# The seven-product form of the up-projection in an encoder block on Trainium2: block products through sums of weights and inputs, the down-projection as a phase of its own

## What is computed

```
h = rms_norm(x, ffn_pre_g[l]) * (1.0 + scale2) + shift2
u = depthwise_conv_centred(h @ w_up[l], conv_w[l], conv_b[l])
a, bval = jnp.split(u, 2, axis=-1)
y = (jax.nn.gelu(a, approximate=True) * bval) @ w_down[l]
x = x + gate2 * rms_norm(y, ffn_post_g[l])
```

## Time and profile before

| | us |
|---|---|
| median of 3 runs | 3207.35 |
| lowest and highest | 3206.72 and 3211.47 |
| profiled execution, span | 3209.9 |

### The profile page before, as it was taken

One profiled execution on the slowest core, in us unless ns is written; L12 is line 12 of the kernel. 1 busy time (PEld: TensorE's weight loads), 2 busy tenths in 40 slices (PEclk: granted clock), 3 DMA queues, 4 the chain that ended last, 5 costly groups with the idle time before them and its releaser, 6 DMA issues.

```text
span 3209.9 us, 35608 instructions
## 1 busy us (share of the span) xinstructions
PE 3146.2 (98%) x14057; PEld 2544.4 (79%) x14057; DVE 2398.0 (75%) x2650; ACT 1274.2 (40%) x1669; POOL 206.1 (6%) x291
## 2 busy tenths in 40 slices
PE   7999999999999999989999999999999999999997
PEld 7777777777788888878888888888888888888886
DVE  5679687774699999986664567676778677777778
ACT  4433111112899999944333422222223322122123
POOL 0011431441000000000000000000000000000001
PEclk8999999999999999999999999999999999999999
DMA  8633333215411121277777221221217111111123
GB/s 321 214 145 131 122 111 109 86 63 194 154 37 37 34 55 39 73 209 215 234 226 266 95 64 49 58 61 46 64 43 256 49 58 49 43 64 43 43 64 126
DMA packets 140806, 349.34 MB, mean 109 GB/s; under 512 B 27192, under 2 KB 36408, under 8 KB 136152
## 3 DMA queue, kind: packets, MB, share of 16 engines
q1 hardware_dynamic: 123040, 303.02, 29.8%
q10 hardware_dynamic: 12096, 25.17, 2.2%
q0 software_dynamic: 5504, 18.88, 1.5%
HBM read 249.56 MB, written 92.20 MB: 106 GB/s over the span
## 4 chain that ended last, share of the span: by engine, by line
PE 53%; DMA 2%; DVE 1%; ACT 0%; issue 0%; POOL 0%; POOLq 0%; SPq 0%; ACTq 0%; DVEq 0%
PE second_ps_a L90 12%; PE second_ps_a L92 12%; PE second_ps_a L91 12%; PE second_ps_b L90 6%; PE second_ps_b L92 6%; PE second_ps_b L91 6%; DMA scratch_h<-merge_x 1%; DMA ffn_x<-scratch_x 0%; DMA merge_x<-in_w_out 0%; PE second_ps_b L1753 0%; DMA merge_st_b<-scratch_rec 0%; DVE second_y L2516 0%; POOL second_y L2345 0%; DVE second_y L2472 0%; ACT merge_x L1768 0%
## 5 line engine op out<-in xcount | busy, mean ns | idle before, releaser
L2472 DVE TENSOR_TENSOR second_y<-second_y,second_ps_b 128x512 f32<-128x512 f32 x654 | 443.5, 687 | 209.4 <-PE second_ps_b L92 209.3
L90 PE MATMUL second_ps_a<-second_h_hi,up_wu_hi 128*128 128x512 f32 x1408 | 547.9, 389 | 0.0
L91 PE MATMUL second_ps_a<-second_h_lo,up_wu_hi 128*128 128x512 f32 x1408 | 547.8, 389 | 0.0
L92 PE MATMUL second_ps_a<-second_h_hi,up_wu_lo 128*128 128x512 f32 x1408 | 547.7, 389 | 0.0
L1525 DVE TENSOR_TENSOR att_prob_lo<-att_prob,att_prob_hi 128x1024 fp32r<-128x1024 f32 x256 | 309.9, 1221 | 24.0 <-ACT att_prob_hi L1484 22.8
L92 PEld LDWEIGHTS second_ps_a<-second_h_hi,up_wu_lo 128*128 128x128 f32 x1408 | 264.3, 188 | 54.9
L90 PEld LDWEIGHTS second_ps_a<-second_h_hi,up_wu_hi 128*128 128x128 f32 x1408 | 264.3, 188 | 54.9 <-DVE up_wu_lo L2179 0.2
L91 PEld LDWEIGHTS second_ps_a<-second_h_lo,up_wu_hi 128*128 128x128 f32 x1408 | 264.3, 188 | 54.8
L90 PE MATMUL second_ps_b<-ffn_wd_hi,ffn_g_hi 128*128 128x512 f32 x704 | 274.9, 391 | 1.8 <-DVE second_y L2472 1.8
L92 PE MATMUL second_ps_b<-ffn_wd_hi,ffn_g_lo 128*128 128x512 f32 x704 | 274.6, 390 | 0.0
L91 PE MATMUL second_ps_b<-ffn_wd_lo,ffn_g_hi 128*128 128x512 f32 x704 | 274.6, 390 | 0.0
(11 more groups left out here) (289 smaller groups left out, 6255.0 us busy)
## 6 DMA issues: line engine op xcount, KB each, us to landing
up_w_st<-in_w_up SPq DMA_DIRECT2D x88, 512.0 KB, 5.9
ffn_wd_st<-in_w_dn SPq DMA_DIRECT2D x44, 512.0 KB, 3.6
scratch_gates<-proj_out SPq DMA_DIRECT2D x64, 256.0 KB, 2.0
early_w_st<-in_w_branch SPq DMA_DIRECT2D x32, 512.0 KB, 6.6
merge_gate<-scratch_gates SPq DMA_DIRECT2D x64, 256.0 KB, 4.4
scratch_h<-merge_x ACTq DMA_DIRECT2D x48, 256.0 KB, 3.8
first_raw_lo<-in_w_ada SPq DMA_DIRECT2D x17, 512.0 KB, 6.6
first_raw_lo<-in_w_ada SPq DMA_DIRECT2D x8, 1024.0 KB, 13.6
```

Of the source, the lines that this page charges most:

```text
L90: pe.matmul(out, w_hi, x_hi, start=first, stop=False)
L91: pe.matmul(out, w_hi, x_lo, start=False, stop=False)
L92: return pe.matmul(out, w_lo, x_hi, start=False, stop=last)
L2472: dve.tensor_tensor(at, at, ps_d[:, q % 4, :], ALU.add).then_inc(s_y, 1)
```

## The change

**Seven products.** A pass's result is a 2 x 2 block product: two groups of 128 output channels, two halves of the depth (512 each), two blocks of 512 positions. `UpWeights` and `UpInput` form sums of the blocks: S1 to S4 of the weights, T1 to T4 of the input. Seven products of 4 depth steps (`product`, 7 x 4 x 3 = 84 matmuls) take the place of eight.

**Weights.** The four sums are made by POOL in every pass, 128 x 512 each (`wu.add`). The seven blocks are split in four groups: A (A11 and A12), S12, S34 and LAST (A22). There is one buffer for the split weights: a group for the next pass is written when this pass's last product that reads it is done (`USED_BY`). The raw weights also have one buffer: SP loads those of the next pass when all four groups of this pass are split.

**Input.** `h` goes through DRAM as one part. The T sums and the splits of the seven input blocks are made once for each half: for the first while the mixing phase ends and in pass 0, by DVE, ACT and POOL (four sums and seven splits of 128 x 2048), for the second in pieces during the first down-projection phase.

**Results.** The seven products are put together: ACT copies two (P1, P5), DVE adds five from PSUM (`take_u2`, `take_c11`, `take_u3`, `take_c12`, `take_c21`), POOL adds two in SBUF (`take_u4`, `take_c22`). `take_c12` waits for POOL's `take_u4`. The first tap of the convolution goes from DVE to ACT (`tap`).

**Down-projection.** The gated values are stored to DRAM (`store_g`). After the 22 passes of a half its down-projection runs in blocks of 4, 3 (first half), 3, 3 and 3 tiles (second half). A block has 11 groups; a group takes two chunks of 128 channels, with two loads of `w_dn` of 512 KB, two loads of gated values, and 12 matmuls for each tile. PSUM keeps the sum over a whole block, so `add_tile` goes. `norm_tile` reads PSUM; its result and `x1` have rings of two buffers, and their stores and loads are issued by POOL.

```diff
+    A11, S1, S2, A12, S3, S4, A22 = range(7)
+    MANY = 7
+    A, S12, S34, LAST = range(4)
+    GROUP_OF = (A, S12, S12, A, S34, S34, LAST)
+    SLOTS_OF = (slice(0, 4, 3), slice(1, 3), slice(4, 6), slice(6, 7))
+    USED_BY = (3, 2, 5, 6)
+    GROUPS = 4
...
+    def load(self, sp, i):
+        if i == NP:
+            sp.wait_ge(self.s_dlo, 2 * NP)
+        elif i:
+            sp.wait_ge(self.s_lo, self.GROUPS * i)
+        for j in range(2):
+            sp.dma_start(self.st[:, j, :], self.w_up[2 * (i % NP) + j]).then_inc(self.s_w, 16)
...
+    def add(self, pool, i, o):
+        s2 = self.sum_of(i, self.S2)
+        at = self.sum_of(i, o)
...
+        if o == self.S1:
+            pool.tensor_tensor(at, self.raw(1, 0), self.raw(1, 1), ALU.add).then_inc(self.s_sum, 1)
+        if o == self.S2:
+            pool.wait_ge(self.s_sum, 4 * i + 1)
+            pool.tensor_tensor(at, self.sum_of(i, self.S1), self.raw(0, 0), ALU.subtract).then_inc(self.s_sum, 1)
+        if o == self.S3:
+            pool.tensor_tensor(at, self.raw(0, 0), self.raw(1, 0), ALU.subtract).then_inc(self.s_sum, 1)
+        if o == self.S4:
+            pool.wait_ge(self.s_sum, 4 * i + 2)
+            pool.tensor_tensor(at, self.raw(0, 1), s2, ALU.subtract).then_inc(self.s_sum, 1)
...
+    def low(self, dve, i, g):
+        dve.wait_ge(self.s_hi, self.GROUPS * i + g + 1)
+        if g == self.S12:
+            dve.wait_ge(self.s_sum, 4 * i + 4)
+        slots = self.SLOTS_OF[g]
+        dve.tensor_tensor(self.lo[:, slots, :], self.source(i, g), self.hi[:, slots, :], ALU.subtract).then_inc(self.s_lo, 1)
+
+    def ready(self, pe, i, o):
+        pe.wait_ge(self.s_lo, self.GROUPS * i + self.GROUP_OF[o] + 1)
...
+        def store_g(i):
+            half, c, v = i // NP, i % NP, i % 2
+            first, to = (1, 0) if half == 0 else (0, HALF - 1)
+            many = HALF - first if half == 0 else NCV
+            sp.wait_ge(s_glo, i + 1)
+            for part, g in enumerate((g_hi[v], g_lo[v])):
+                sp.dma_start(g_d[c, part, :, to:to + many], g[:, first:first + many].bitcast(F32)).then_inc(s_gst[v], 16)
...
+        def load_dn(m):
+            half = half_of_group(m // 2)
+            if m - 2 * first_group(half) < 2:
+                sp.wait_ge(wu.s_lo, wu.GROUPS * NP * (half + 1))
+            else:
+                sp.wait_ge(s_dlo, m - 1)
+            sp.dma_start(wd_st[:, m % 2, :], w_dn[m % NP]).then_inc(s_wd[m % 2], 16)
...
+        def load_g(n):
+            half, gr = half_of_group(n), n % GR
+            b, v = n // GR, ring(n)
+            if n - first_group(half) == 1:
+                sp.wait_ge(s_gst[0], 32 * (NP // 2) * (half + 1))
+            if n - first_group(half) >= 2:
+                sp.wait_ge(s_dn, down_done(n - 1))
+            for a in range(2):
+                sp.wait_ge(s_gst[a], 32 * ((NP // 2) * half + gr + 1))
+            first, many = BLOCKS[b][0] * P, len(tiles(b)) * P
+            for a in range(2):
+                sp.dma_start(gs[v][:, a, :, 0:many].bitcast(F32),
+                             g_d[2 * gr + a, :, :, first:first + many].rearrange("h p s -> p h s")).then_inc(s_gl[v], 16)
...
+            load_dn(2 * first_group(half) + 2)
+            load_dn(2 * first_group(half) + 3)
+            store_g(last)
+            load_g(first_group(half) + 1)
+            sp.wait_ge(s_gst[1], 32 * (NP // 2) * (half + 1))
...
+            for n in groups(half):
+                k = n - first_group(half)
+                if k and n + 1 in groups(half):
+                    load_group(n + 1)
...
+                wu.load(sp, NP)
...
         def load_x1(t):
...
+            if t - 2 > (LAST_TILE[0] if t > LAST_TILE[0] else -1):
+                pool.wait_ge(s_o, t - 1)
+            pool.dma_start(x1[:, in_ring(t), :], x1_d[t]).then_inc(s_x[in_ring(t)], 16)
+
+        def store(t):
+            pool.wait_ge(s_o, t + 1)
+            pool.dma_start(out_d[t], yw[:, in_ring(t), :]).then_inc(s_ost[in_ring(t)], 16)
+
+        def take_u4(i):
+            pool.wait_ge(s_p5, i + 1)
+            pool.wait_ge(s_u3, i + 1)
+            pool.tensor_tensor(u2[:], u2[:], p5[:], ALU.add).then_inc(s_u4, 1)
...
+            for i in range(NP * half, NP * (half + 1)):
...
+                    for o in wu.SUMS:
+                        wu.add(pool, i + 1, o)
+                take_u4(i)
+                take_c22(i)
...
+            for t in range(first, last + 1):
+                if half == 0 and t == last - 2:
+                    for o in wu.SUMS:
+                        wu.add(pool, NP, o)
+                if t < NT - 1:
+                    store(t)
+                if t + 2 <= last:
+                    load_x1(t + 2)
...
+        def norm_of_block(b):
+            for t, spot in zip(tiles(b), BLOCKS[b][1]):
+                act.wait_ge(s_dn, down_done(GR * b + GR - 1) + t - tiles(b)[0] + 1)
...
+                act.activation(junk[:].rearrange("p (c q) -> p c q", q=BLK), down_of[spot], ACT.Square,
+                               accum_out=sums[:, t:t + 1]).then_inc(s_sq, 1)
+                act.wait_ge(s_sq, t + 1)
+                act.activation(std[:, t:t + 1], sums[:, t:t + 1], ACT.Sqrt, bias=eps[:, 0:1], scale=1.0 / D).then_inc(s_std, 1)
...
+        def pass_of(i):
+            c = i % NP
+            if c:
+                wu.high(act, i, wu.LAST)
+                tap(i - 1, 1)
+            copy_p1(i)
+            if c:
+                gelu(i - 1)
+            if i == 0:
...
+            copy_p5(i)
...
+            if c:
+                high_g(i - 1)
...
+            if c < NP - 1:
+                for g in (wu.A, wu.S12, wu.S34):
+                    wu.high(act, i + 1, g)
...
+            tap(i, 0)
...
+        def take_u2(i):
...
+            dve.tensor_tensor(u2[:], bank_of(i, P6), p1[:], ALU.add).then_inc(s_u2, 1)
...
+        def take_u3(i):
+            dve.wait_ge(s_up, wu.MANY * i + P7 + 1)
...
+            dve.tensor_tensor(u3[:], bank_of(i, P7), u2[:], ALU.add).then_inc(s_u3, 1)
+
+        def take_c12(i):
+            dve.wait_ge(s_up, wu.MANY * i + P3 + 1)
+            dve.wait_ge(s_u4, i + 1)
+            dve.tensor_tensor(u[:, 0, 2 + BLK:2 + HALF], bank_of(i, P3), u2[:], ALU.add).then_inc(s_c12, 1)
...
-        def add_tile(i, t):
...
-                dve.wait_ge(s_dn, q + 1)
-                dve.tensor_tensor(at, at, ps_d[:, q % 4, :], ALU.add).then_inc(s_y, 1)
...
+            dve.scalar_tensor_tensor(cv[:, j, :], u[:, j, 1:NCV + 1], one(1), cv[:, j, :], ALU.mult, ALU.add).then_inc(s_cs, 1)
...
+            dve.scalar_tensor_tensor(cv[:, j, :], u[:, j, 2:NCV + 2], one(2), cv[:, j, :], ALU.mult, ALU.add).then_inc(s_cd, 1)
...
+        def low_g(i):
+            dve.wait_ge(s_ghi, i + 1)
+            dve.tensor_tensor(g_lo[i % 2][:], cv[:, 0, :], g_hi[i % 2][:], ALU.subtract).then_inc(s_glo, 1)
...
+        def norm_tile(t, spot):
+            at = yw[:, in_ring(t), :]
...
+            if uses(t):
+                dve.wait_ge(s_ost[in_ring(t)], 16 * uses(t))
+            if t < NT - 1:
+                dve.scalar_tensor_tensor(at, down_of[spot].rearrange("p c q -> p (c q)"), rstd[:, t:t + 1], g2[:], ALU.mult, ALU.mult)\
+                    .then_inc(s_n, 1)
+                dve.wait_ge(s_n, t + 1)
+                dve.wait_ge(s_x[in_ring(t)], 16 * (uses(t) + 1))
+                dve.tensor_tensor(at, at, x1[:, in_ring(t), :], ALU.add).then_inc(s_o, 1)
...
+                norm_tile(t, spot)
+
+        def pass_of(i):
+            c = i % NP
+            half = i // NP
+            if c:
+                take_c21(i - 1)
+                wu.low(dve, i, wu.LAST)
+                convolve(i - 1, 0)
+                if half:
+                    halo(i, 0)
+                convolve(i - 1, 1)
+                if half:
+                    halo(i, 1)
+                times(i - 1)
+            elif half:
...
+            take_u2(i)
+            if c:
+                low_g(i - 1)
+            take_c11(i)
...
+            more = c < NP - 1
+            if more:
+                wu.low(dve, i + 1, wu.A)
...
+            take_u3(i)
...
+            take_c12(i)
+            if more:
+                wu.low(dve, i + 1, wu.S12)
+                wu.low(dve, i + 1, wu.S34)
...
+        def product(i, q):
+            n, many = wu.MANY * (i % NP) + q, len(RINGS[i // NP])
+            wu.ready(pe, i, q)
...
+            if n >= many:
+                before, of = divmod(n - many, wu.MANY)
+                pe.wait_ge(S_TAKEN[of], NP * (i // NP) + before + 1)
...
+            for k in range(KH):
+                cols = slice(k * P, (k + 1) * P)
+                m = product3(pe, at, wu.hi[:, q, cols], wu.lo[:, q, cols], th.hi[q][:, k, :], th.lo[q][:, k, :],
+                             k == 0, k == KH - 1)
+            m.then_inc(s_up, 1)
...
+        def down(n):
+            b, gr, v = n // GR, n % GR, ring(n)
+            half = half_of_group(n)
+            pe.wait_ge(s_dlo, 2 * n + 2)
```

(9 more changed lines are left out.)

1015 lines of the change are left out of this document (523 added, 492 removed).

## The result

The changed kernel takes 3191.1 us (median of 4 runs, 3185.1 to 3195.6) beside 3209.4 us for the kernel before (3206.7 to 3212.3). The ratio is 0.9938, with a 95% interval of 0.9922 to 0.9954: it is faster by 0.6%, where 1.5% was forecast. The profiled span is 3193.8 us.

What follows compares the result with a forecast made beforehand. PE was taken to bound the kernel before, a loop without PE the new passes. 3209.9 - 119 (matmuls) - 8 (tail) + (6 + 16 + 8 + 6 + 10) (seams, clock) + 34 (loop) = 3163, less 2.5: 3160 us; range 3118 to 3222.

Steps and rivals of the forecast that it cites:

- Matmuls: Up-projection passes: 44 passes lose 12 matmuls each, 528 x 0.2257 = 119 us less.
- tail: From PE's last matmul to the end about 10 us; with the 1.8 us stall and its slow matmuls gone, -8.
- passes 22 and 23: Between the halves: the output ring delays LAST of pass 22 and the loads for pass 23; 6 us, high end 12.
- The loop: Weight splits, loads, sums and c12, without PE: 19.8 us a pass, 0.84 over PE's 18.96; 34 us over 40 passes.
- Rival 1: Up-projection passes: PE bounds, loop 18.96 us or less, 3126 us in all; chance 0.22.
- rival 2: Up-projection passes: DVE and POOL block each other for full instruction lengths, loop 20.8 us, 3200 us in all; chance 0.15.
- Rival 3: Up-projection passes: six DVE-POOL meetings instead of four and later loads, loop 22 us, slower at 3248 us; chance 0.13.
- First pass: Start of the up-projection: last x1 some 8 us later, T3's split behind it, PE waits 6 us; high end 12.
- Round trips: Start of each down-projection: gated values through DRAM arrive late for group 1, 6.7 + 9.4 = 16 us; high end 24.
- Ends of blocks: Three block ends: third tile's output waits for the first's store, DVE splits w_dn late; 8 us, high end 15.
- Clock: Slow matmuls behind five stalls longer than 2 us, at 2 us each: 10 us.
- Rival 4: Down-projection: transfers late by 1 us in each of 55 groups, 3215 us in all; chance 0.07.

Runs made afterwards that it cites:

- e3: Changed kernel, but at block ends DVE normalises the third and fourth tile only behind the next weight splits (also ahead of pass 22); 3172.7 us.
- e10: Changed kernel plus a POOL write of 128 x 1536 zeros, reading nothing, behind c22 in 34 passes, beside DVE's splits; 3187.6 us.
- e1: Changed kernel with the sum u4 in a buffer of its own in passes 2 to 20 of each half, no longer waiting for u3; 3163.0 us.
- e9: Changed kernel plus e4's POOL addition in the same 34 passes, but held until DVE's second tap, so beside DVE's taps; 3240.4 us.
- e4: Changed kernel plus one unneeded POOL addition of 128 x 512 behind c22 in 34 passes, beside DVE's splits; 3228.7 us.
- e7: Changed kernel with first-pass work reordered: POOL's first weight sums and DVE's T3 split earlier, the last block's transposes later in pass 1; 3185.5 us.
- e13: Changed kernel with the sum T4 done by DVE behind its split of B22 instead of by POOL; 3192.0 us.
- e2: Changed kernel with a third ring buffer for gated values, loaded ahead of the last stores, for group 1 and the second half's odd groups; 3190.7 us.
- e11: e5 with both new buffers at round addresses, and w_dn's splits and group 2's loads moved ahead at the end of each half; 3158.8 us.
- e12: Changed kernel with the edits of e1, e3, e6, e7 and e11 together, and further reordering of sums and transposes around pass 1; 3108.2 us.
- e5: e2 with the gate rows loaded behind group 4's loads and two new buffers for the second half, at + 0 and + 32; 3175.9 us.
- e6: Changed kernel with the first ring buffer of gated values at 196 KiB instead of 196 KiB + 64, three tiles moved for room; 3182.7 us.

## Why the prediction missed

- **Matmuls, tail, passes 22 and 23:** right to 1 us each, and e3, which loses 0.5 instead of 5.8 in pass 23, shows the cause of that term. DVE's additions to the running sum were free, as said.
- **The loop:** right in its mechanism and size. 19.8 was forecast; 19.84 is the common pass and 19.4 one in five. e10's trace shows what the shorter one is: the product starts 0.15 us ahead of S1 and isn't blocked (1.23 us), and POOL's sums are. Its parts are there: pair landing 4.9 (5.0), the conflict, and c12 behind u4, which e1 shows to be the link that sets it. (The prediction's terms add to 17.8 us without the conflict, not 17.9; the forecast doesn't hang on it.) Rival 1 (PE bounds) was wrong for this kernel and right for e1; rival 2's 20.8 was wrong since a blocked instruction loses 1.1, not 1.29 us, and some meetings don't happen. Rival 3's path is real: e9 makes one meeting more, has a loop of 21 to 21.6 and is slower than the kernel before (1.0085). So is e4 with 20.95: with the seams as they are the gain is gone at about 19.84 + 18.3/40 = 20.3, not at 21.0.
- **First pass, 6 us, high end 12: the step that failed most.** The seam measured 24. The prediction followed one order of work on DVE to the last x1 and T3, and the wait that it named is there: 5.1 us for T3, though the last x1 comes 14 us later than before and not 8 (1769.5 against 1755.4), 3.1 of it by the two engines' conflict, which the same text had just derived. The other 18 lie in what it left out: two waits of 1.6 and 1.5 us in pass 0; pass 1's transposes, whose rows DVE scales only at the end of its list for pass 0 (5.2); ACT, which empties the transposes' two PSUM banks only behind the gelu and the split of g (4.3); and slow matmuls behind the longer of these. e7 and e13 show that removing one late item only shows the next; what each cause alone is worth stays open.
- **Round trips, 16, high end 24: mis-sized;** 21.4 of waits and about 5.5 of slow matmuls, which the prediction had under the clock. The wait was at the forecast place, and the loads were issued a little earlier than forecast; the step that failed is their landing, up to 8.9 and 6.9 us after issue, right behind the last stores, instead of 4.5. That group 2's loads stand behind SP's 7 us for the stores' own landing was left out; it became the stall when group 1's had gone (e2). (The terms listed add to 17.8 us, not 17.5.)
- **Ends of blocks, 8, high end 15:** right place, 13 of waits; the third tile waits for the x1 load too, and the fourth of block 0 for a store of its own.
- **Clock, 10:** 12, behind the five stalls over 2 us in the down-projections; some 2.5 each instead of 2.
- **Pitch, not in the sum:** 7.5. The earlier trace rows gave the distance of matmuls of another placement of tiles.
- **Rival 4** (late transfers in the down-projection) didn't occur: 227 GB/s in the window, and no wait for the ring but at group 1.

The seams were five terms of 6 to 16 us, each at its likeliest value, and four came out above; their high ends together (12 + 24 + 15 + 12, and 10 for the clock) would have given a span of 3190. The first passes alone came out at twice their high end. That is the error to learn from: terms that all hang on one busy engine or on the same transfers missed in the same direction.

## What to carry to other kernels

Where a change shortens the bound engine's work, write down the loop that doesn't pass through that engine and look for a sum that overwrites its own input; giving it a buffer may be worth more (28 us here) than the whole change had gained (18). List for each in-order queue what stands behind each of its waits, those of loads that nobody needs yet included, before pricing a seam. Place the tiles that TensorE loads as weights at round addresses (3% of a matmul here).

## What the runs showed of the hardware

The windows of the changed kernel after the stall of 10.37 us at group 1, and behind it:

```profile
2235.00:2240.00 5.00, 5.00 (x12) 3.87 (x13) 0.16 (x1) 1.06 (x1) 0.00 (x0) 0.50 0.95 343
2240.00:2245.00 5.00, 5.00 (x23) 4.14 (x22) 2.29 (x2) 1.06 (x1) 0.00 (x0) 1.00 1.03 398
...
3096.00:3100.00 4.00, 3.91 (x17) 3.23 (x18) 0.04 (x1) 0.00 (x0) 0.00 (x0) 1.00 0.92 266
```

- Behind a stall of 10.4 us PE ran at 1.2 GHz (granted clock 0.50) for 5 us with 12 matmuls, then at full clock: 2.3 us lost. Behind one of 1.70 us (3096) it kept full clock, where the kernel before lost it behind 1.80. The length of the stall alone doesn't decide it: behind 1.76 us the clock was 0.57 in the next 3.4 us (e10, 3095.6), behind 2.04 us it was 1.00 (e11, 3063.4) and behind 2.21 us too (e12, 1802.3).
- The place of the stationary tile sets the distance of matmuls: 0.2266 us at + 0, 0.2334 at + 32 and + 64 (e5, e6).
- POOL writing 128 x 1536 without reading doesn't disturb DVE's splits (2.75 us for two with and without it, e10); an addition of 128 x 512 on POOL costs a split 1.10 us (e4) and a tap 1.13 (e9).
- A load of 512 KB, 3.6 us to landing in the median of w_dn's, took 7.9 and 8.9 right behind two stores of 512 KB (2225.34).
- The up-projection began between 1745.1 us (e1) and 1753.3 (e13) from one profiled run to another, though the instructions ahead of it are the same in these, so spans were compared stage by stage.
